# Value units of a transformer block computed by features with all 272 tokens as columns and turned back; meta products of the differential attention put side by side

## The reference

```python
u = rms_norm(h, pre_mix_gain[l])
proj = u @ w_in[l]
qa, ka, va, qb, kb, vb, g = jnp.split(proj, SPLITS, axis=-1)
...
va = va.reshape(B, Lp, SWA_KV_HEADS, HEAD_DIM)          # 4 heads of 64
vb = vb.reshape(B, Lp, DIFF_HEADS, DIFF_V_DIM)          # 8 heads of 128
o_swa = windowed_gqa_sink_attention(qa, ka, va, attn_sink[l], pos, is_real)
...
s = jnp.einsum('bqhcd,bkhcd->bhcqk', qi, k).astype(jnp.float32) * scale + key_bias
p = jax.nn.softmax(s, axis=-1)
a = (p[:, :, 0] - lam * p[:, :, 1]).astype(v.dtype)
return jnp.einsum('bhqk,bkhe->bqhe', a, v)
```

## Time and profile before

| what | value |
| --- | --- |
| median of 3 runs | 1029.18 us (1025.25 to 1031.27) |
| the profiled execution | 1029.06 us |
| its span, first to last instruction | 1027.1 us |
| mean granted clock of TensorE | 0.989 |
| TensorE / VectorE / ScalarE / GpSimd busy | 96% / 66% / 52% / 11% |
| HBM read | 150.76 MB, 150 GB/s over the span |

### The profile page before, as it was taken

How to read it: one execution, slowest core, us unless ns; L and a number is a source line. 1 busy time by engine, 2 the same in 40 slices (tenths; PEclk the granted TensorE clock), 3 DMA queues, 4 the chain that set the end, 5 groups by cost and what they waited for, 6 DMA issues and landing times.

```text
span 1027.1 us, 16819 instructions
## 1 busy us (share of the span) xinstructions
PE 990.1 (96%) x6844; PEld 898.0 (87%) x6844; DVE 682.8 (66%) x1242; ACT 537.1 (52%) x1034; POOL 116.3 (11%) x141
## 2 busy tenths in 40 slices
PE   6999999999999999999999999899999999999997
PEld 6889999888898988888889998888799998888886
DVE  5666556566648866767657568975755467667674
ACT  6656565565445654444446685564444354434443
POOL 1111101011102200000001108811100000000001
PEclk9999999999999999999999998899999999999999
DMA  9333233323434755555565562210244165554541
GB/s 319 123 127 123 84 124 123 117 96 118 171 130 158 229 198 205 175 195 195 180 219 181 173 233 88 82 42 1 88 166 158 56 211 198 172 205 164 205 164 42
DMA packets 126108, 154.99 MB, mean 151 GB/s; under 512 B 2728, under 2 KB 117680, under 8 KB 125648
## 3 DMA queue, kind: packets, MB, share of 16 engines
q1 hardware_dynamic: 123616, 142.91, 41.2%
q0 software_dynamic: 1952, 10.61, 2.9%
q10 hardware_dynamic: 464, 0.40, 0.2%
HBM read 150.76 MB, written 3.16 MB: 150 GB/s over the span
## 4 chain that ended last, share of the span: by engine, by line
PE 78%; DVE 9%; ACT 9%; issue 2%; DMA 1%; POOL 0%; POOLq 0%; DVEq 0%; ACTq 0%
PE ps L759 13%; PE ps L760 7%; PE ps L1040 6%; PE ps L735 5%; PE ps L737 5%; PE ps L736 5%; PE ps L779 5%; PE ps L781 4%; PE ps L780 4%; PE ps L1013 4%; PE ps L1014 3%; PE ps L1015 3%; ACT whi L1927 3%; PE ps L726 3%; DVE wlo L1279 2%
## 5 line engine op out<-in xcount | busy, mean ns | idle before, releaser
L1279 DVE TENSOR_TENSOR wlo<-raw,whi 128x1024 fp32r<-128x1024 f32 x268 | 325.3, 1230 | 236.4 <-ACT whi L1927 235.7
L1927 ACT ACTIVATE whi<-raw 128x1024 fp32r<-128x1024 f32 x268 | 274.4, 1050 | 153.0 <-PE ps L760 53.9
L759 PE MATMUL ps<-R1b,whi 128*128 128x512 f32 x576 | 201.8, 393 | 0.0
L760 PE MATMUL ps<-R1b,wlo 128*128 128x256 f32 x576 | 161.6, 281 | 0.0
L735 PE MATMUL ps<-R1b,whi 128*128 128x256 f32 (+1 forms) x512 | 152.0, 297 | 0.0
L736 PE MATMUL ps<-R1b,whi 128*128 128x256 f32 (+1 forms) x512 | 146.7, 287 | 0.0
L737 PE MATMUL ps<-R1b,wlo 128*128 128x256 f32 (+1 forms) x512 | 146.6, 286 | 0.0
L759 PEld LDWEIGHTS ps<-R1b,whi 128*128 128x128 f32 x576 | 108.2, 188 | 24.7 <-issue 0.5
L760 PEld LDWEIGHTS ps<-R1b,wlo 128*128 128x128 f32 x576 | 108.4, 188 | 0.6
L735 PEld LDWEIGHTS ps<-R1b,whi 128*128 128x128 f32 x512 | 99.0, 193 | 8.8 <-issue 6.0
L736 PEld LDWEIGHTS ps<-R1b,whi 128*128 128x128 f32 x512 | 98.8, 193 | 0.4 <-issue 0.2
(11 more groups left out here) (294 smaller groups left out, 2108.7 us busy)
## 6 DMA issues: line engine op xcount, KB each, us to landing
raw<-in_w_in SPq DMA_DIRECT2D x35, 1024.0 KB, 5.0
raw<-in_w_ffn_in SPq DMA_DIRECT2D x22, 1024.0 KB, 5.0
raw<-in_w_ffn_out SPq DMA_DIRECT2D x11, 1024.0 KB, 5.3
raw<-in_w_gate SPq DMA_DIRECT2D x11, 1024.0 KB, 5.1
raw<-in_w_up SPq DMA_DIRECT2D x11, 1024.0 KB, 5.2
raw<-in_w_down SPq DMA_DIRECT2D x11, 1024.0 KB, 5.5
raw<-in_w_out SPq DMA_DIRECT2D x8, 1024.0 KB, 5.2
raw<-in_w_xkv SPq DMA_DIRECT2D x8, 1024.0 KB, 5.6
```

The source lines that it names most:

```text
L759: e.matmul(B[:, :].rearrange("p (a n) -> p a n", a=2), hi[:, kt, c], R[2][:, :, kt, 0:256], start=kt == 0, stop=False)
L760: m = e.matmul(B[:, 0:256], lo[:, kt, c], R[0][:, kt, 0:256], start=False, stop=kt == 7)
L1279: e.tensor_tensor(half_of(wlo[i % HL], i, k), half_of(raw[i % RAW], i, k), f32(half_of(whi[i % HL], i, k)), SUB).then_inc(lo_split(i, (i, k)))
L1927: return e.activation(o, i, f, **kw)
```

## The change

The value units take the form "feat": each half is 128 features by all 272 tokens. ScalarE copies each half to a buffer `VT` (two of them, one for each half), TensorE turns it with three transposes (two of 128 tokens, one of 16) into a bank of the heads, and VectorE copies it to the places where the values stood before (for "va" the meta part four times, for half the columns each). The turn of the first half stands in the plan right behind the second half; that of the second half stands behind the first half of the next unit (`behind`). The products with the values wait for VectorE's copy alone. As all units from va on are "feat" or alike, `alike` changes its answer: it becomes true between a value unit and the units two before and two after it, and false between unit 2 and unit 0. In the differential attention the four products with real tokens (two query tiles by two key tiles) now come first, then the two with the meta tokens.

```diff
--- before.py
+++ after.py
@@ -316,7 +316,23 @@
             yield 1
 
     def values(key, col0, u):
-        return unit(("v", key, u), "w_in", "tok", col0 + 256 * u)
+
+        order.append(("w_in", "feat", col0 + 256 * u, 256))
+        i = len(order) - 1
+        for j in range(2):
+            take(i, j)
+            step("v", key, u, j, i)
+            if j:
+                step("vt", key, u, 0)
+            yield 1
+
+    def behind(work, *steps):
+
+        next(work)
+        for s in steps:
+            step(*s)
+        yield 1
+        yield from work
 
     def gates(u):
         return unit(("gate", u), "w_in", "feat", 4608 + 256 * u)
@@ -333,6 +349,8 @@
     qa, qb, kb, vb = [[rope(k, c, u) for u in range(4)] for k, c in (("qa", 0), ("qb", 1536), ("kb", 2560))] + [
         [values("vb", 3584, u) for u in range(4)]]
     ga, bs = [gates(u) for u in range(8)], [branch_swa(u) for u in range(4)]
+    qa[1] = behind(qa[1], ("vt", "va", 0, 1))
+    kb = [behind(kb[u], ("vt", "vb", u, 1)) for u in range(4)]
     units = [opening(), rope("ka0", 1024, 0), values("va", 1280, 0), qa[1], ga[0], qa[2], ga[1], qa[3], ga[2], qb[0], vb[0], kb[0],
              ga[3], qb[1], vb[1], kb[1], ga[4], qb[2], vb[2], kb[2], ga[5], qb[3], vb[3], kb[3], ga[6], *bs, ga[7]]
     at = []
@@ -473,7 +491,7 @@
         set_dve, set_act = signal("set_dve"), signal("set_act")
         norm_pe, norm_act, norm_dve, norm_pool = [signal("norm_" + n) for n in ("pe", "act", "dve", "pool")]
         rope_act, rope_dve, rope_pool = [signal("rope_" + n) for n in ("act", "dve", "pool")]
-        val_act, val_dve = signal("val_act"), signal("val_dve")
+        val_pe, val_act, val_dve = [signal("val_" + n) for n in ("pe", "act", "dve")]
         swap_act, gate_act = signal("swap_act"), signal("gate_act")
         head_pe, head_act, head_dve, head_pool = [signal("head_" + n) for n in ("pe", "act", "dve", "pool")]
         merge_act, merge_dve, merge_pool = [signal("merge_" + n) for n in ("act", "dve", "pool")]
@@ -554,6 +572,7 @@
         VB = F[:, 8192:11264].rearrange("p (t n) -> p t n", t=3)
         ROPE = {"qa": (QA, 256), "ka0": (KA, NT), "qb": (QB, 256), "kb": (KB, NT)}
         VAL = {"va": VA, "vb": VB}
+        VT = [SD[:, 512:512 + NT], SD[:, 2560:2560 + NT]]
         E2 = [SC[:, 1088 * i:1088 * (i + 1)].rearrange("p (u n) -> p u n", u=4) for i in range(2)]
         PT = [SC[:, 2176 + 512 * i:2688 + 512 * i] for i in range(2)]
         MC, MT = SC[:, 3200:3328], SC[:, 3328:3456]
@@ -861,14 +880,17 @@
                         m = e.matmul(o, lo[:, kt, c], R1[0][:, kt, 0:256], start=False, stop=kt == 7)
                 m.then_inc(gemm(("half", i, part), ("unit", i), ("rope", 0), ("rope", 1)))
 
-            def v(key, u, part, i):
-                if part == 0:
-                    claim("gemm", (key, u), (val_act, (key, u)))
-                    claim("gemm", (key, u, "m"), (val_dve, (key, u)))
-                    p.wait_ge(norm_dve, ("n1", "lo", 8))
-                B, M = ps(key, u), ps(key, u, "m")
-                tok(i, part, R1, 256, normed("n1"), (B[:, 0:256], 0, 128, True, (key, u, 0)),
-                    (B[:, 256:512], 128, 128, False, (key, u)), (M[0:16, 0:256], 256, 16, True, (key, u, "m")))
+            def v(key, u, j, i):
+                B = claim("gemm", (key, u, j), (val_act, (key, u, j)))
+                p.wait_ge(norm_dve, ("n1", "lo", 8))
+                feat(B[:, 0:NT], i, j, R1, NT, normed("n1"), (key, u, j))
+
+            def vt(key, u, j):
+                B = claim("head", (key, u, j, "t"), (val_dve, (key, u, j)))
+                p.wait_ge(val_act, (key, u, j))
+                for t in range(2):
+                    tr(B[:, 128 * t:128 * t + 128], VT[j][:, 128 * t:128 * t + 128])
+                tr(B[0:16, 256:384], VT[j][:, 256:NT]).then_inc(val_pe((key, u, j)))
 
             def scores(x, t, Q, K, done):
                 for c in range(2):
@@ -902,8 +924,7 @@
                     tr(B[:, 256:384], MC).then_inc(head_pe(("M", x)))
                 if part == "v":
                     O = ps("O", x)
-                    p.wait_ge(val_act, ("va", 0))
-                    p.wait_ge(val_dve, ("va", 0))
+                    p.wait_ge(val_dve, ("va", 0, kv // 2))
                     p.wait_ge(head_dve, ("meta", x))
                     e.matmul(O[:, 0:256], MT, VM[:, kv, :, :], start=True, stop=False)
                     for t in range(2):
@@ -945,16 +966,17 @@
                     m.then_inc(head_pe(("PT", x), ("M", x)))
                 if part == "v":
                     O, P = ps("O", x), PT[copies(x)[0]]
-                    p.wait_ge(val_act, ("vb", h // 2))
-                    p.wait_ge(val_dve, ("vb", h // 2))
+                    p.wait_ge(val_dve, ("vb", h // 2, h % 2))
                     p.wait_ge(head_act, ("PT", x))
                     p.wait_ge(head_dve, ("meta", x))
                     for t in range(2):
                         for kt in range(2):
                             e.matmul(O[:, 128 * t:128 * t + 128], P[:, 256 * kt + 128 * t:256 * kt + 128 * t + 128],
-                                     VB[:, kt, 128 * h:128 * h + 128], start=kt == 0, stop=False)
-                        e.matmul(O[:, 128 * t:128 * t + 128], MD[:, 128 * t:128 * t + 128], VB[0:16, 2, 128 * h:128 * h + 128],
-                                 start=False, stop=True).then_inc(head_pe(("V", x)))
+                                     VB[:, kt, 128 * h:128 * h + 128], start=(t, kt) == (0, 0), stop=False)
+                    for t in range(2):
+                        m = e.matmul(O[:, 128 * t:128 * t + 128], MD[:, 128 * t:128 * t + 128], VB[0:16, 2, 128 * h:128 * h + 128],
+                                     start=False, stop=t == 1)
+                    m.then_inc(head_pe(("V", x)))
                 if part == "t":
                     turn_out(x)
 
@@ -1255,7 +1277,7 @@
                                          PX[h % 2][:, 256 * k:256 * k + 256], start=k == 0, stop=k == 1)
                     m.then_inc(cross_pe(("xo", h)))
 
-            parts = {"turn": turn, "turnx": turnx, "rsb": rsb_, "rope": rope, "ropek": ropek, "turnm": turnm, "v": v, "swa": swa, "diff": diff, "gate": gate, "bsw": bsw, "bdf": bdf,
+            parts = {"turn": turn, "turnx": turnx, "rsb": rsb_, "rope": rope, "ropek": ropek, "turnm": turnm, "v": v, "vt": vt, "swa": swa, "diff": diff, "gate": gate, "bsw": bsw, "bdf": bdf,
                      "out": out_, "mem": mem, "upg": upg, "upu": upu, "down": down, "tail": tail, "conv": conv, "zg": zg,
                      "delta": delta, "dsa": dsa, "dsah": dsah, "xq": xq, "cross": cross}
             for now[0], (name, *a) in enumerate(plan):
@@ -1365,17 +1387,18 @@
             def roped(key, b, k):
                 rope(key, b, 0, 0, k)
 
-            def v(key, u, part, i):
-                if part:
-                    d.wait_ge(gemm, (key, u, "m"))
-                    M = ps(key, u, "m")[0:16, 0:256]
-                    if key == "vb":
-                        e.tensor_copy(VB[0:16, 2, 256 * u:256 * u + 256], M).then_inc(val_dve((key, u)))
-                    else:
-                        d.wait_ge(head_pool, "zero")
-                        for q in range(4):
-                            e.tensor_copy(VM[32 * q:32 * q + 16, :, q, :], M.rearrange("p (k d) -> p k d", k=4)).then_inc(
-                                val_dve((key, u)))
+            def vt(key, u, j):
+                B = ps(key, u, j, "t")
+                d.wait_ge(val_pe, (key, u, j))
+                c = slice(256 * u + 128 * j, 256 * u + 128 * j + 128)
+                e.tensor_copy(VAL[key][:, 0:2, c], B[:, 0:256].rearrange("p (t n) -> p t n", t=2)).then_inc(val_dve((key, u, j)))
+                if key == "vb":
+                    e.tensor_copy(VB[0:16, 2, c], B[0:16, 256:384]).then_inc(val_dve((key, u, j)))
+                else:
+                    d.wait_ge(head_pool, "zero")
+                    for q in range(4):
+                        e.tensor_copy(VM[32 * q:32 * q + 16, 2 * j:2 * j + 2, q, :],
+                                      B[0:16, 256:384].rearrange("p (k d) -> p k d", k=2)).then_inc(val_dve((key, u, j)))
 
             def swa(g, part):
                 x = nth["swa", g]
@@ -1913,7 +1936,7 @@
 
             e.memset(half, -0.5).then_inc(set_dve("half"))
             e.memset(ones, 1.0).then_inc(set_dve("one"))
-            parts = {"split": split, "rows": rows, "turn": turn, "turnx": turnx, "stat": stat_, "rsb": rsb_, "chunk": chunk, "chunk2": chunk2, "upg": upg, "setup": setup, "rope": rope, "roped": roped, "turnm": turnm, "v": v, "swa": swa, "diff": diff,
+            parts = {"split": split, "rows": rows, "turn": turn, "turnx": turnx, "stat": stat_, "rsb": rsb_, "chunk": chunk, "chunk2": chunk2, "upg": upg, "setup": setup, "rope": rope, "roped": roped, "turnm": turnm, "vt": vt, "swa": swa, "diff": diff,
```

(10 more changed lines are left out.)

## The result

| what | before | after |
| --- | --- | --- |
| median of the runs | 1029.63 us (6 runs, 1025.25 to 1031.27) | 1019.72 us (6 runs, 1017.90 to 1020.55) |
| ratio | | 0.9911, 95% interval 0.9894 to 0.9928 |
| the profiled execution, its span | 1029.06, 1027.1 us | 1020.01, 1018.0 us |
| mean granted clock | 0.989 | 0.992 |

The changed kernel is 9.9 us faster by these medians, and 9.1 us faster by the profiled executions. On two further chips, beside other runs of the kernel before, it came out 7.3 us faster each time (1026.59 to 1019.34 and 1026.48 to 1019.21; ratios 0.9928 and 0.9918, intervals 0.9908 to 0.9948 and 0.9893 to 0.9943). The forecast was 1021.0 us.

What follows compares the result with a forecast made beforehand. The prediction took TensorE as the bound, busy 96% of the span with 78% of the chain. Savings less turns and waits summed to -8.1 us, from 1029.06 to 1021.0 us; range 1015.5 to 1025.5.

Steps and rivals of the forecast that it cites:

- eight vb halves: Value units on TensorE: each half drops from 4.31 to 3.11 us, 1.20 us less, 9.6 us for eight.
- eight turns: Three added transposes per half on TensorE, 0.08 us each, 0.24 per half, 1.9 us in all, without waiting for ScalarE.
- meta products: Differential attention, eight heads: grouping the products with meta tokens saves 0.20 us per head, 1.6 us in all.
- first vb half lost at swa 3: The product behind that half waits for VectorE's copy of the meta weights, so its 1.2 us gain is lost.
- diff 3's scores behind vb 3's first half: These scores reuse a bank that an exponential reads until 218.05 us, so 0.6 us of gain is lost.
- key unit behind vb 3: VectorE's copies of the second turn come before the maxima, so TensorE's 0.62 us wait grows; 0.3 us lost.
- wait at 204 us goes: TensorE's 1.33 us wait before scores nearly vanishes because ScalarE's split waits for one half only; 1.2 us gained.
- va unit: At the start, a later split delays the first scores to about 34.5 us; 0.3 lost, between 1.9 gained and 2 lost.
- clock, before 101 and behind 304 us: Early idle time may bring a clock drop of some 1.7 us, mostly hidden; after 300 us only the start changes.
- The bound of 2.4: Upper limit in us for grouping the meta products, if the step between the two meta pairs is 0.11 us too.
- Nearly the whole wait goes: 1.2 us gained: Before the scores at 204.07 us: exponentials 1.9 us earlier, less 0.54 for copies, remove most of TensorE's 1.33 us wait.
- the second rival: ScalarE and VectorE hold the stretch 185 to 235 us, so only 4.6 us is gained, 1024.5 us; chance 0.20.

Runs made afterwards that it cites:

- the values alone: The changed kernel with the old order of the differential attention's products with meta tokens; 1019.41 us, ratio 0.9934 to the kernel before.
- meta products alone: The kernel before with only the differential attention's products regrouped, real tokens first, then meta tokens; 1023.76 us, ratio 0.9969 to the kernel before.

## Why the prediction was right, point by point

The time was 1.3 us under the forecast and inside its range. Its mechanism held in the stretch that TensorE bounds. Behind it, several sizes were off in both directions, and that the total came so close is partly luck: the forecast's own terms came to -6.4 us for -8.1, and the clock, which it put at nothing, gave 2.7 us in the profiled executions.

| term | forecast | in the trace |
| --- | --- | --- |
| eight vb halves | -9.6 | -9.6 (3.10 to 3.14 us each) |
| eight turns | +1.9 | +2.8 (0.33 between transposes, 0.41 ahead of scores) |
| meta products | -1.6 | -3.1 (0.38 or 0.39 in each of the eight heads) |
| scores behind the fourth product | 0 | +0.2 (0.88 for 0.66 us) |
| wait of the first product for VectorE | 0 | -0.1 |
| first vb half lost at swa 3 | +1.2 | +1.2 |
| diff 3's scores behind vb 3's first half | +0.6 | +1.1 |
| key unit behind vb 3 | +0.3 | +0.1 beyond the turn |
| wait at 204 us goes | -1.2 | +0.4 |
| sum from 101 to 312 us | -8.4 | -7.0; the starts say -6.9 |
| va unit | +0.3 | +0.5 |
| clock, before 101 and behind 304 us | 0 | -2.7 |

- *The halves and the loss at swa 3* came as argued: 1.2 us of each half, and none of vb 0's first, whose successor waits 1.03 us for VectorE. With the product moved, the turn waited 1.68 us for ScalarE instead, so this one copy isn't the only limit there.
- *The turns* were never stopped by ScalarE in the changed kernel. Their size failed. One by one, a transpose starts 0.11 us after the one before, and a fp32r matmul 0.03 us after the last transpose. So two cost 0.14 us and six 0.57, but each further one costs 0.11, and I had taken the 0.08 of an average. A turn that stands ahead of other transposes costs three times 0.11, 0.33 us.
- *The meta products* were mis-sized: I took 0.21 us for each step between two meta products, from pairs in which the first step follows a change of the row count. Four in a row take 0.21, 0.11, 0.11 and 0.20, so the full step belongs to the change alone. The bound of 2.4 was too low: per head 0.38 us, two changes less, 0.19 each, 3.1 us in all. Only 2.1 of them arrive (6.9 us for both parts less 4.8 for the values alone): 0.8 is lost in the two waits at 200 and 214 us, and 0.2 in the scores behind the fourth product, where an exponential ends at 241.47 and the score matmul behind it starts at 241.61. The Trainium skill's TensorE: Matmul & The Clock Gate, section Single matmul latency, gives a drain of some 175 ns; the estimate of 0.35 us per head that the prediction worked out from it is close to the 0.38 of the trace.
- *"Nearly the whole wait goes: 1.2 us gained"* is the step that failed. ScalarE's wait for the half did go, as argued. But VectorE has no idle time from 178.08 to the maxima at 182.51: a split (180.84) still stands ahead of them, and now the first turn's copies, which the prediction left out here. The exponentials start 3.45 us behind the scores at 180.06, where before it was 3.74: 0.3 us earlier, not the 1.9 of the prediction. The second turn's copies take 0.54 back one set of maxima later, so the scores at 199.62 stand 19.56 us behind those at 180.06, for 19.31 before. With the values alone the wait is what it was before (1.32 for 1.33), and the +0.4 of the table is the saving of the first diff product, lost in it. Without the copies on VectorE they stand 18.48 us behind, 0.8 less than before, so the copies are most of what was missing. That was the mechanism of the second rival: from 180 to 228 us the forecast's terms come to about -2.6 us and the rival's to +0.7, and -1.0 was measured (48.37 for 49.33 us).
- *Diff 3's scores* waited for the bank that ScalarE's exponentials read, as argued; it is 1.1 us, nearly the whole half. With the values alone 0.7 us of the half is lost there (14.12 us from the scores before, where the kernel before took 14.58), for 0.6 forecast; the other 0.4 is what the second diff product saves, which the forecast counted as gained.
- *va*: +0.5 for +0.3 forecast, scores of swa 0 at 35.24 for 34.5, of which 0.57 is unit 0's later end.
- *The clock.* The profiled executions happened to differ: -1.5 at 68 to 72 us, +0.57 at the start (the last section), +1.5 in the product with the output weights (18.93 us for 17.43), and -3.2 behind it, where before has more time at half clock. Most of it comes and goes between executions of one kernel: two of the changed kernel reach the scores of swa 0 at 35.24 and 33.15 us. One part may belong to the change: of the three profiled executions with va by tokens two had the drop at 68 us, of the eleven with va by features none, and all eleven had one near 35 us, most of which a wait covers. The runs don't settle it. With the sizes measured, the forecast's own terms give -6.4 us (-6.9 and +0.5), and -7.3 was measured with equal clocks; the 0.9 us between them, which a drop of 1.4 us in two executions of three would make, stays open.
- *The chances* of the prediction don't add up as it words them: 0.56, 0.10, 0.10 and a quarter of 0.20 are 0.81, not 0.79.

## What to carry to other kernels

When TensorE is the bound, count a saved instruction at its pitch and then walk through the places where TensorE meets the other two engines: what is saved just ahead of such a place is lost there in part or whole, and that holds for every part of a change, also for the small ones that stand ahead of somebody else's wait. At such a place, a wait that the profile gives to ScalarE may be VectorE's queue one step further back; look at what stands ahead of the maxima, and move copies to the engine that idles there, not to a later place in the same queue. Read the price of a step from a run of equal steps: the first after a change of form carries the cost of the change.

## What the hardware showed that I had not expected

- The change between 128 and 16 rows of weights costs TensorE about 0.1 us at either side; four products of 16 rows in a row cost 0.11 us each inside the run.
- Three transposes cost 0.24 us between fp32r matmuls (44.56 to 44.80), 0.33 ahead of other transposes and 0.41 ahead of the scores with 64 rows: the step from the last one is 0.03, 0.11 or 0.20 us.
- In unit 0, the distance between matmuls of 256 columns goes from 0.21 to 0.12 us at 17.1 us in the kernel before and at 18.6 in the one after, and in a second execution of the latter at 13.9 us, with the same instructions. The views give a clock of 1.00 ahead of these points too, but the list of clock changes in the packed traces begins only there, with full speed at 17.28, 18.61 and 13.69 us, so that 1.00 is no reading. The kernel after runs 1.33 us longer at 0.21 than the one before, and 1.33 x (1 - 0.12 / 0.21) is 0.57 us, the later end of unit 0 (an estimate).
- Behind 300 us, where all these kernels do the same work, the mean clock of a stretch of 10 us falls to 0.83 or less (time at 1.2 of 2.4 GHz) at two to four of the same four places, beginning at 304 to 319, 612 to 627, 643 to 657 and 676 to 686 us; which of them, and for how long, differs between executions. In the product with the output weights such a drop costs 1.5 us (18.93 for 17.43), one twice as long 2.5 (19.89, meta products alone). The runs of one kernel are spread over 2 to 9 us.
